# A two-block transformer on one core: the hybrid mixer's work put in another order, by numbered steps, with its decay chain on GpSimd

## The reference

```python
def hybrid_mixer(x, ...):
    proj = x @ w_in + b_in
    (qa, ka, va, beta_raw, a_raw, za, qb, kb, vb, qc, kc, vc) = jnp.split(proj, split_at, axis=-1)
    o_a = gated_deltanet(qa, ka, va, beta_raw, a_raw, za, conv_w, a_log, dt_bias, gdn_norm_g)
    o_b = chunk_relpos_attention(qb, kb, vb, rel_bias)
    o_c = swa_sink_attention(qc, kc, vc, sinks)
    gates = jax.nn.sigmoid(x @ w_gate + b_gate).reshape(b, t, N_BRANCH, d)
    merged = (gates[:, :, 0] * (o_a @ w_br_a) + gates[:, :, 1] * (o_b @ w_br_b)
              + gates[:, :, 2] * (o_c @ w_br_c))
    return merged @ w_out
# gated_deltanet: a causal convolution of four taps and silu on q, k, v; q and k l2-normalised;
# beta = sigmoid(beta_raw); g = -exp(a_log) * softplus(a_raw + dt_bias); a delta rule with the
# decay exp(cumsum g); its output rms-normalised, times norm_g * silu(za)
# x = layer_norm(alpha * x + mix) follows
```

## Time and profile before

| | us |
|---|---|
| median of three runs | 2519.02 |
| the profiled execution | 2520.33 |
| its span (first to last instruction) | 2518.5 |
| PE busy | 2411.8 (96%) |
| VectorE busy | 1801.2 (72%) |
| ScalarE busy | 1299.5 (52%) |
| GpSimd busy | 114.4 (5%) |

### The profile page before, as it was taken

How to read it: one execution, slowest core, us unless ns; L and a number is a source line. 1 busy time by engine, 2 the same in 40 slices (tenths; PEclk the granted TensorE clock), 3 DMA queues, 4 the chain that set the end, 5 groups by cost and what they waited for, 6 DMA issues and landing times.

```text
span 2518.5 us, 38940 instructions
## 1 busy us (share of the span) xinstructions
PE 2411.8 (96%) x15814; PEld 2202.9 (87%) x15814; DVE 1801.2 (72%) x2683; ACT 1299.5 (52%) x1989; POOL 114.4 (5%) x104
## 2 busy tenths in 40 slices
PE   8699999999999999889998999999998899989998
PEld 7688889888888888889998888988888899988887
DVE  6679657679768866766468876687668664688765
ACT  5555454545445544556445554455444664455543
POOL 0012000002100000210000000000002100000000
PEclk9899999999999999989999999999999899999999
DMA  6246565446556665533345656465654333446662
GB/s 218 75 142 207 181 212 170 134 139 203 177 176 209 192 186 175 170 109 101 101 151 162 198 185 183 159 209 185 187 188 156 105 105 101 160 142 202 185 180 87
DMA packets 114883, 409.92 MB, mean 163 GB/s; under 512 B 12817, under 2 KB 14993, under 8 KB 114705
## 3 DMA queue, kind: packets, MB, share of 16 engines
q1 hardware_dynamic: 114704, 407.43, 50.6%
HBM read 406.33 MB, written 1.05 MB: 162 GB/s over the span
## 4 chain that ended last, share of the span: by engine, by line
PE 86%; DVE 9%; ACT 3%; issue 1%; DMA 0%; POOL 0%; SPq 0%; ACTq 0%; DVEq 0%
PE ps L365 85%; DVE wlo L1702 3%; ACT whi L1048 1%; ACT region L1214 1%; PE ps L586 0%; DVE H L1720 0%; DVE x L1861 0%; DVE x L1879 0%; DVE region L1904 0%; DVE region L2001 0%; DMA cst<-in_consts 0%; DVE region L2296 0%; DVE region L2293 0%; DVE region L2252 0%; DVE region L1907 0%
## 5 line engine op out<-in xcount | busy, mean ns | idle before, releaser
L365 PE MATMUL ps<-xx,whi 128*128 128x256 f32 (+1 forms) x4920 | 1343.7, 344 | 27.1 <-ACT region L1450 16.1
L1702 DVE TENSOR_TENSOR wlo<-raw,whi 128x1024 fp32r<-128x1024 f32 (+3 forms) x772 | 936.2, 1217 | 444.2 <-ACT whi L1048 442.5
L1048 ACT ACTIVATE whi<-raw 128x1024 fp32r<-128x1024 f32 (+3 forms) x772 | 801.6, 1043 | 548.6 <-PE ps L365 541.7
L365 PE MATMUL ps<-xx,wlo 128*128 128x256 f32 x3696 | 1045.2, 283 | 0.0
L365 PEld LDWEIGHTS ps<-xx,whi 128*128 128x128 f32 x4920 | 862.6, 192 | 143.3 <-ACT region L1450 16.5
L365 PEld LDWEIGHTS ps<-xx,wlo 128*128 128x128 f32 x3696 | 707.8, 191 | 0.3
L365 PE MATMUL ps<-H,whi 128*128 128x512 f32 (+1 forms) x2400 | 684.4, 350 | 19.6 <-DVE wlo L1702 10.4
L365 PE MATMUL ps<-H,wlo 128*128 128x256 f32 x1888 | 533.6, 283 | 0.0
L365 PEld LDWEIGHTS ps<-H,whi 128*128 128x128 f32 x2400 | 424.6, 191 | 83.8 <-issue 15.8
L365 PEld LDWEIGHTS ps<-H,wlo 128*128 128x128 f32 x1888 | 358.4, 190 | 0.2
L1697 DVE TENSOR_REDUCE t<-ps 128x256 f32<-128x512 f32 x308 | 211.5, 688 | 51.8 <-PE ps L365 42.9
(11 more groups left out here) (276 smaller groups left out, 1528.2 us busy)
## 6 DMA issues: line engine op xcount, KB each, us to landing
raw<-in_sg SPq DMA_DIRECT2D x128, 512.0 KB, 4.3
raw<-in_su SPq DMA_DIRECT2D x128, 512.0 KB, 4.3
raw<-in_sd SPq DMA_DIRECT2D x128, 512.0 KB, 4.4
raw<-in_mw_g SPq DMA_DIRECT2D x48, 512.0 KB, 3.4
raw<-in_fg SPq DMA_DIRECT2D x44, 512.0 KB, 3.4
raw<-in_fu SPq DMA_DIRECT2D x44, 512.0 KB, 3.3
raw<-in_fd SPq DMA_DIRECT2D x32, 512.0 KB, 3.6
raw<-in_mw_a SPq DMA_DIRECT2D x24, 512.0 KB, 4.2
```

The lines of the kernel that those rows point to most:

```text
L365: return e.matmul(out, lhsT, rhs, start=start, stop=stop, skip_group_check=True)
L1048: e.activation(m.whi[:, c % NHL, 0:cw], m.raw[:, c % NRAW, 0:cw], ACT.Copy).then_inc(s["whi"].h, s["whi"].up(c))
L1702: e.tensor_tensor(m.wlo[:, c % NHL, 0:cw], m.raw[:, c % NRAW, 0:cw], m.whi[:, c % NHL, 0:cw].bitcast(F32), ALU.subtract).then_inc(s["wlo"] ...
```

## The change

In the hybrid mixer of both layers:

- **Order of chunks.** After `mw_c`: the output gate values `mw_z`, the last four of `mw_a`, the values `mw_v` (with the columns laid out so that the c values, beta and a come in the first half), then `mw_qkb`. Branch c's eight gate chunks come in a row, ahead of its four products; b and a stay as they were.
- **Numbered steps.** A generator says at which step it goes on (`yield from side.at(n)`), by tables; step 0 is the first `mw_z` chunk. Attention c's first four heads start at 9, the others at 18, attention b at 27. In the first block's attention the former counts stand as `relative(...)`.
- **Norm ahead of values.** Roots at steps 8 to 10, the four nt products at 10 to 12 through banks 4 and 5, key transposes at 12 and 13, value transposes at 17.
- **Raw tiles.** VectorE's lowering stands ahead of each `raw`; query chunks go through banks 0 to 3; the small bias operation waits no more for `rowc`; ScalarE does four raw tiles first and the others between its reads of the query chunks.
- **Convolution.** All three further taps on VectorE, none on GpSimd; its silus are spread over steps 2 to 10.
- **Decay.** The series runs on GpSimd, VectorE keeps the reciprocals, ScalarE does |x|, relu and exp.
- **End.** The projection uses banks 2, 3, 4, 5, 0, 1, 6, 7; one `chunk()` stands ahead of tile 2; sums and squares from tile 1 on come after tile 7 (`late`).
- Attention b's outputs are put out in pairs of heads, the c gates go straight into the merge buffer.

```diff
@@ weight_order
-        o += [(f"mw_v{l}", i) for i in range(6)] + [(f"mw_a{l}", i) for i in range(8, 12)]
-        o += [(f"mw_qkb{l}", i) for i in range(8)] + [(f"mw_z{l}", i) for i in range(4)]
-        for br in (2, 1, 0):
+        o += [(f"mw_z{l}", i) for i in range(4)] + [(f"mw_a{l}", i) for i in range(8, 12)]
+        o += [(f"mw_v{l}", i) for i in range(6)] + [(f"mw_qkb{l}", i) for i in range(8)]
+        o += [(f"mw_g{l}", 16 + i) for i in range(8)] + [(f"mw_br{l}", 8 + p) for p in range(4)]
+        for br in (1, 0):
@@ Sides
+    def at(self, n):
+        while self.n <= n:
+            yield
...
+ROUNDS = {("c", 0): 9, ("c", 4): 18, ("b", 0): 27}
+PE_PARTS = {"s0": 0, "s1": 1, "t0": 5, "t1": 6, "p0": 7, "p1": 7}
+ACT_PARTS = {"e0": 2, "e1": 3, "t0": 5, "t1": 6, "p0": 7, "p1": 7}
+DVE_PARTS = {"s0": 1, "s1": 2, "m": 2, "n": 5, "p0": 8, "p1": 8}
@@ tensor_program, hybrid
-            gemm_fm(f"mw_c{l}", i, take(i % 2, ("pact", l, "c", i))[:, 0:256], xh, xl)
+            gemm_fm(f"mw_c{l}", i, take(i % 4, ("pact", l, "c", i))[:, 0:256], xh, xl)
...
+            for p in range(4):
+                yield from side.at(10 + p // 2)
+                w.wait_ge(s["ddve"], l, "in", "r")
+                b = take(pe4[p % 2], ("ddve", l, "nt", p))
...
+            for n in range(2):
+                yield from side.at(12 + n)
+                w.wait_ge(s["ddve"], l, "nt", 3)
...
+        for i in range(4):
+            gemm_fm(f"mw_z{l}", i, take(4 + i % 2, ("pact", l, "z", i))[:, 0:256], xh, xl)
+            side.step()
@@ vector_program, hybrid
         for i in range(6):
-            raw(m.pr[i], ps[i], i, ((f"mw_a{l}", i), (l, i)), pk(f"bqa{l}", i))
             if i < 4:
                 produce(1, 4)
+            raw(m.pr[i], ps[i], i, ((f"mw_a{l}", i), (l, i)), pk(f"bqa{l}", i))
...
+            for p in range(4):
+                yield from side.at(11 + p // 2)
                 v = m.cv[:, 2 * p:2 * p + 2, :]
                 w.wait_ge(s["dps"], l, "nt", p)
...
         for n in range(8):
-            norm_tile(f"t{l}", (f"l2g{l}", f"l2b{l}"), n, 3, add_one, (f"mw_o{l}", n), n)
-            if n >= 3:
+            if n == 2:
+                chunk()
+            norm_tile(f"t{l}", (f"l2g{l}", f"l2b{l}"), n, 3, add_one, (f"mw_o{l}", n), m.mo_bank[n], late=True)
+            if 3 <= n < 7:
                 chunk()
@@ gpsimd_program, hybrid (the taps are gone)
+        then(e.tensor_tensor(f24(m.W0), m.BA[:, :, 4:8], row("dt").unsqueeze(1).broadcast_to([128, 2, 4]), ALU.add), "dt")
+        w.wait_ge(s["sdve"], l, "y2")
+        then(e.tensor_tensor(W1, W1, W3, ALU.mult))
+        then(e.tensor_tensor(W2, W1, W1, ALU.mult))
+        then(e.tensor_scalar(W3, W2, 2.0 / 17, 2.0 / 15, ALU.mult, ALU.add))
+        for cf in (13, 11, 9, 7, 5, 3, 1):
+            then(e.tensor_tensor(W3, W3, W2, ALU.mult))
+            then(e.tensor_scalar(W3, W3, 2.0 / cf, None, ALU.add))
```

More of the change, by code:

```diff
@@ L330 @@
     "pdve",
-    "cpool",
     "cdve",
+    "spool",
     "sdve",
@@ L1441, in hybrid @@
             tap(i)
-        for i in range(6, 8):
+        for i in range(4):
+            produce(1, 4)
+            raw(i)
+        for _ in range(2):
             chunk()
-            taps(i)
         for i in range(5):
@@ L1580, in delta @@
                     e.activation(h2[0][:, k, :], o_[:, k, :], ACT.Copy).then_inc(s["hhi"].h, s["hhi"].up("a", l, k))
-                yield
             flag.add("A")
+        side.n = 0
+        side.add(convs())
+        side.add(decay())
+        side.add(delta())
+        side.add(both())
+        for i in range(4):
+            chunk()
+            w.wait_ge(s["gemm"], f"mw_z{l}", i)
+            e.activation(m.zf[:, i, :], ps[4 + i % 2][:, 0:256], ACT.Silu, bias=pk(f"bza{l}", i)).then_inc(
+                s["pact"].h, s["pact"].up(l, "z", i))
+            side.step()
+        for i in range(8, 12):
+            chunk()
+            taps(i, 6 + i % 2)
+            side.step()
+        for _ in range(6):
+            chunk()
+            side.step()
         for i in range(8):
@@ L1831, in norm_tile @@
         elif n == 7:
-            squares(st, 6)
+            for k in range(1 if late else 7, 7):
+                total(st, k, nz)
+            for k in range(1 if late else 6, 7):
+                squares(st, k)
             if st != "end":
@@ L2015, in attend @@
                     s["advc"].h, s["advc"].up("z", tag, h0))
-            for _ in range(gap):
-                yield
+            yield from go(h0, "n")
             w.wait_ge(s["aact"], "e", tag, h0 + 3, 1)
@@ L2396, in decay @@
+            yield from side.at(18)
             w.wait_ge(s["sact"], l, "eg")
-            then(e.tensor_tensor(f8(m.BG), f8(m.EG), f8(m.BE), ALU.mult), "bg")
-            flag.add("sm")
-        side.add(decay())
-        for i in range(8, 12):
-            chunk()
-            if i > 8:
-                conv(i - 1)
-            side.step()
+            w.wait_ge(s["sdve"], l, "be")
+            e.tensor_tensor(f8(m.BG), f8(m.EG), f8(m.BE), ALU.mult).then_inc(s["sdve"].h, s["sdve"].up(l, "bg"))
@@ L2518, in delta @@
                     low(h2[1][:, k, :], m.cv[:, 8 + k, :], h2[0][:, k, :], ("hhi", "hlo"), "a", l, k)
-                yield
             flag.add("A")
+        side.n = 0
+        side.add(decay())
+        side.add(delta())
+        side.add(both())
+        for i in range(4):
+            chunk()
+            if i < 3:
+                conv(5 + i)
+            side.step()
+        for i in range(8, 12):
+            chunk()
+            if i > 8:
+                conv(i - 1)
+            side.step()
+        for i in range(6):
+            chunk()
+            if i == 0:
+                conv(11)
+            if i == 1 and l == 0:
+                w.wait_ge(s["lvm"], "in")
+                e.tensor_copy(m.lvm[:, :, :], m.lvf).then_inc(s["set"].h, s["set"].up("lvm"))
+            if i == 3:
+                value(0)
+            side.step()
         for i in range(8):
@@ L2539, in branch @@
             for p in range(4):
-                chunk()
-                side.step()
-                chunk()
-                side.step()
+                gates()
                 if br == 0 and p:
```

667 lines of the change are left out of this document (318 added, 349 removed).

## The result

The changed kernel is slower. Its median is 2535.48 us (2534.41 to 2539.21) where the kernel before, beside it, took 2519.2: ratio 1.0065 (95% interval 1.0048 to 1.0083). The forecast was 2505 in 2470 to 2522. It was wrong, and by its sign.

The account below looks back on a forecast made before the run. The matmul engine (PE), busy 96% of the span, was taken as the bound, so only its waits could be won. Terms -2 x 4.9 + 12.4 - 2 x 8.6 = -14.6 us gave 2505 us, range 2470 to 2522.

Parts of the forecast that it names:

- the middle: Values to the last step before merging: 13.0 us of waits, 20.4 with clock per layer, together +12.4 over both.
- the merging part keeps its margin: Merging of the inverse, where PE waited for nothing before: no new wait, costed at nothing.
- my charge of 2.1 for each longer wait: Clock loss added for every PE wait of 2 us or longer: 2.1 us more each.
- key transposes: Step 12, between values and merging: PE waits 2.9 us for VectorE's fourth norm product.
- second half: Step 22, chunk pair L/A of the second half: PE waits 3.7 us for its first factor.
- score transposes: Step 14, between values and merging: PE waits 2.5 us for the normalised scores, where 5.1 was.
- gate values: Gate values (z), four sharing two banks: PE waits 2.0 us for ScalarE's first read.
- The c stretch: First narrow matmul chunk to last attention-query chunk: idle 4.2 instead of 8.05, half a clock loss; 4.9 us less per layer.
- The end: Last product to last output-projection chunk: waits go, 0.3 may show for late sums; 8.6 us less per layer.
- GpSimd's chain: Decay between steps 13 and 16: 21 dependent operations at 0.35, 7.4 us, hidden with 3.9 to spare.
- rival 2: Slower: the decay on GpSimd, at contended means, is 11.7 us late per layer; 2533 us, chance 0.11.
- three signs of being wrong: A PE wait released by GpSimd; no middle wait over 1.5 us; an end stretch still longer than 25 us.

Follow-up runs that it names:

- copies: The changed kernel with VectorE's predicated copies of each triangular-inverse level one step earlier, beside the products they read; ratio 1.0019.
- both: The changed kernel with the attentions' side work ahead of the decay's and the delta rule's in a step, on all three engines; ratio 1.0017.
- b_c: The kernel before with only the changed kernel's stretch from first narrow matmul chunk to last attention-query chunk; ratio 1.0000.
- pool: The changed kernel with 39 more 8-element multiplications in GpSimd's decay chain; ratio 1.0141, 2556.79 us.
- b_end: The kernel before with only the mixers' end changed: projection banks, a chunk lowered ahead of tile 2, late sums; ratio 0.9933.
- again: The changed kernel rerun unaltered; its rival B said the slow stretch ahead of the first mixer belongs to the program; 2534.7 us, ratio 1.0041.
- mult: The changed kernel with VectorE's side work ahead of the multiply in the third branch's four product steps; ratio 1.0024.

## Why the prediction was wrong

**The step that failed** is half a sentence at the end of the middle: "the merging part keeps its margin". I had costed it at nothing, naming no work that hides it. The copies stood a step later in the diff, and two paragraphs earlier I had written the rule that prices this: side work of a step on VectorE can't start before about 2.2 us into the chunk. The third copy, which PE waits for, then ends at 4.1 with copies 0.6 us apart, and PE asks after 2.9: at least 1.2 late. Measured were 1.96 to 2.88, since the lowering ended 3.0 to 3.4 us into the chunk and not at 2.2 (at the first wait ScalarE's exponentials stand ahead of its rounding), and the multiply of a product, 0.6, stands ahead in two of three. With three such waits and two smaller ones the merging part lost 9.3 us of waits in each layer and some of the clock (0.99 and 0.98 where it was 1.00): summed over windows of 0.5 us, 1.7 us in layer 0 and 3.4 in layer 1. That is 11.0 and 12.7, together 23.7 of the 30.0 us between forecast (14.6 off) and profile (15.4 on).

The copies' step is one part of what took the margin, the order within a step another. With the copies alone moved back the second attention's softmax, which runs last in a step, made PE wait in their place (*copies*, 10.6 us of waits and clock in layer 0 for 11.0); the order alone left the copies late (*both*); the two together came to 8.0. Of the 6.3 us of waits in these, 4.1 are for that softmax. No run removed them, so what else holds them is open.

**The middle** was forecast to lose 12.4 us over both layers. What is left of the losses of 16.6 and 19.8 is 5.6 and 7.1, 12.7. The match is partly luck, for two terms were off against each other. The waits came to 11.8 and 11.5 us a layer where 13.0 was said. The clock cost 12.0 and 10.2 by the granted clock (6.8 and 8.5 in the kernel before), where my charge of 2.1 for each longer wait gave 7.4. The single waits are mixed: key transposes 4.6 (2.9 said), second half 3.1 (3.7), score transposes 1.2 (2.5), squares 1.2 (0.7), gate values 1.75 (2.0), the last none (1.2). The mechanism of the largest is as told. ScalarE, whose table load and exponentials stand ahead of a rounding, waits 6.72 for the maxima:

```profile
1100.06 1.28 ACT L1241 ACT_TABLE_LOAD   x1 [6.72 <-DVE region L2058]
1101.35 0.21 ACT L1241 ACTIVATE region<-region 128x8 f32<-128x8 f32 x1
...
1103.22 1.04 ACT L1069 ACTIVATE whi<-raw 128x1024 fp32r<-128x1024 f32 x1
```

and VectorE, idle for that rounding, multiplies the norm product last:

```profile
1104.29 1.23 DVE L1727 TENSOR_TENSOR wlo<-raw,whi 128x1024 fp32r<-128x1024 f32 x1 [4.31 <-ACT whi L1069]
1105.43 1.28 DVE L2422 SCALAR_TENSOR_TENSOR region<-region,ps 128x512 f32<-128x512 f32 x2
```

The first activation again follows its table load at once (1100.06 + 1.28); the longer price per switch of the Trainium skill (ScalarE: Activation LUTs, "What ACT_TABLE_LOAD costs"), weighed in the prediction, does not show here. It does not show ahead of a load either: the one at 1238.67 starts 0.02 us after ScalarE's instruction before it ended.

**The c stretch** was right: 5.7 and 5.9 off where 4.9 was said. The waits are 1.27, 1.27 and 0.77 behind a first of 0.2 (0.35, 1.45, 1.45, 0.9), and the stretch's granted clock is 1.00, so the half of a clock loss that I took was too much (and the lower end of 2.8 that I gave does not follow from my terms: 10.2 - 4.2 - 2.1 is 3.9). What I had not seen is that the gain depends on the order behind it (*b_c*).

**The end** was right, and a size in it wrong. It takes 9.4 and 9.7 less; with 8.9 said ahead of the sums that is near. The sums take longer than I said, as they depend on one another:

```profile
1346.93 2.55 DVE L1872 TENSOR_TENSOR R<-R,x 128x256 f32<-128x256 f32 x5
1349.40 3.07 DVE L1880 TENSOR_TENSOR t<-t 128x256 f32<-128x256 f32 x6
```

0.51 each, 6.0 for twelve, where I had 0.36 from three independent operations and 4.3. PE waited 2.19 for them, and the stretch behind the end grew by 2.6 and 2.4 us where 0.3 was said: 4.4 us of the miss.

**GpSimd's chain**, the rival that gave 2533, cost nothing, though the time came out at its figure. 21 operations took 9.4 us, 0.45 each with what lies between (0.35 said, threshold 0.54). Most took 0.20, some far more:

```profile
1109.57 0.20 POOL L2678 TENSOR_TENSOR region<-region 128x8 f32<-128x8 f32 x1
...
1110.75 1.23 POOL L2681 TENSOR_TENSOR region<-region 128x8 f32<-128x8 f32 x1
...
1117.43 1.29 POOL L2688 TENSOR_SCALAR region<-region 128x8 f32<-128x8 f32 x1
```

A time that agrees with a rival proves nothing; the waits named none by GpSimd, and *pool* showed what one would look like.

**The chances.** Slower stood at 0.13, and the bounds of the range at 2522, since I had given no case in which a part that I took at nothing went wrong. All my ends were ends of terms in the sum, and rival 2, with its 2533 and its chance of 0.11, lay outside the range. Of the three signs of being wrong that I named none came, though the forecast was wrong: all three looked at terms that I had costed.

## What to carry to other kernels

When a change renumbers steps, list for each producer and consumer the step before and after, and price each one that moved by the floor that holds within a step (here a lowering, then the side work in its order); a part whose matmuls are the same is not thereby a part whose waits are. Take a gain in one stretch together with the stretch behind it, since the wait removed may only move there (*b_c*), and give "this part stays as it is" a chance of its own to be wrong. When the result comes, ask the waits, not the total: the total agreed with a rival whose wait was nowhere.

## What the hardware showed that was not expected

**The same instructions at another pace.** Between 160 and 340 us both kernels run the same matmuls with the same single wait of 1.3 us at the same clock, but PE gets through fewer. The kernel before, then the changed one, then the run again:

```profile
160.00:340.00 180.00, 178.73 (x1016) 155.68 (x1015) 144.60 (x210) 93.41 (x131) 26.58 (x22) 1.00 0.63 199
```

```profile
160.00:340.00 180.00, 178.73 (x1005) 154.92 (x1004) 143.81 (x209) 92.91 (x130) 26.69 (x22) 1.00 0.61 194
```

```profile
160.00:340.00 180.00, 178.99 (x1003) 155.01 (x1002) 143.51 (x208) 92.58 (x129) 26.66 (x22) 1.00 0.62 195
```

1016 against 1005 is 1.1%, some 2 us. *b_c* shows 1016, *copies* 1010, *both* 1013, *b_end* 1005. In the two profiles of the changed kernel PE ends its first wait of the c stretch at 1032.57 and 1032.51 us, 0.06 apart, so rival B of *again* came out; in *copies*, *both* and *mult*, run on the same chip as *again*, it is 1028.37, 1029.38 and 1031.92. So the pace seems to go with the program rather than with the chip or the execution (two profiles of one program are all there is for it); what in the program sets it no run here tells. Together with one more stretch at half clock, at 534 to 538 us, it is the 4.6 us lost ahead of the mixer. That is 30% of the profile's 15.4 us, in a part that the change was not aimed at, and it blurs every comparison of programs here by up to 0.2%.

**Small gaps and the clock.** Three gaps of 1.27, 1.27 and 0.77 us within 10 us of the c stretch left the granted clock at 1.00, where the stretch with the one gap of 8.0 had 0.83. A small gap is not always without cost: in the middle of the same layer one of 1.18 us, with 32 matmuls of one column behind it, was followed by 0.54 from 1080.2 to 1087.7.

**Eight elements on GpSimd.** An operation that takes 0.20 us there, 0.29 from start to start, took 0.17 on VectorE in this trace, 0.20 to 0.21 from start to start. In direction this agrees with the Trainium skill (GPSIMD Engine Reference, section 4.1, "Engine selection"), which prefers VectorE; the factor of two that it states does not show for so few elements (1.4 from start to start).
